# The third set of chain tiles moves from a place of the weight ring into two landing buffers

## The chip, the cores and the metric

The kernel runs on one core of one Trainium2 chip. The metric is device time in microseconds (us) of one execution, the median of the runs shown. TensorE is PE in the rows (PEld is its weight load), VectorE is DVE, ScalarE is ACT, GpSimd is POOL and SyncE is SP; SPq is SyncE issuing DMAs.

## The reference

Two transformer-like blocks over 256 tokens of width 2048, all in float32: attention and convolution with a gated FFN first, then a layer of stick-breaking attention and pooling, then an RWKV-7 layer. The change lies in the last layer, where the projection `g` is computed while the recurrence runs:

```python
r = (xr @ w_r).astype(f32)
k = (xk @ w_k).astype(f32)
v = (xv @ w_v).astype(f32)
g = (xg @ w_g).astype(f32)
...
def step(state, inp):
    r_t, w_t, k_t, v_t, kk_t, a_t = inp
    sa = jnp.einsum('bhvk,bhk->bhv', state, -kk_t)
    state = (state * w_t[:, :, None, :]
             + sa[..., None] * (kk_t * a_t)[:, :, None, :]
             + v_t[..., None] * k_t[:, :, None, :])
    return state, jnp.einsum('bhvk,bhk->bhv', state, r_t)
...
o = ((o - mean) * lax.rsqrt(var + GN_EPS)).reshape(B_, S, D) * gn_w + gn_b
bonus = jnp.sum(r * k * r_k, axis=-1, keepdims=True) * v
o = (o + bonus.reshape(B_, S, D)) * jax.nn.silu(g)
return o.astype(x.dtype) @ w_o
```

## The kernel before

**Units.** All weight matrices are streamed through one pipeline in the order of `ORDER`. A unit is a block of 512 rows by 256 columns of a weight, 512 KB, and there are 760. Four units in a row of the same 256 columns make a slab of `w_g`. The units of `w_v` end at 695, `w_g` is 696 to 727 (slabs of four: 696 to 699, 700 to 703 and so on), `w_o` is 728 to 759. `W1` is 696, the first unit of `w_g`.

**A unit's way.** SyncE lands it in one of the landing buffers `raw0` to `raw2` with two DMAs of 256 KB (line 542, in `sync_program`). ScalarE rounds it to a high part `wH` (line 573), VectorE subtracts to get the low part `wL` (`wL = raw - wH`, line 1168), and TensorE multiplies both parts with the activations. I call the ScalarE and the VectorE step together the split of a unit. A landing buffer may be filled again when both steps of the unit that it held are done: `sync_program` waits on the counts `hi` and `lo`. `wH` and `wL` form a ring of four places (`RING`), and a split has to wait until TensorE has finished the unit that held the place (`unit`).

**Who splits what, when.** Each engine runs a program written in the order of the units. At unit `u` ScalarE and VectorE first call `split(u)`, which covers the units from `SPLIT[u - 1]` to `SPLIT[u]`; then they do their part of the scan. With the full ring, `split(u)` covers unit `u + 3`. All five queues are in order, so an engine that waits at a split does nothing that stands behind it.

**The scan.** The recurrence runs as three interleaved chains of jobs and norms (`_chains`, `job`, `norm`, `turn`), spread over the `w_g` units: TensorE puts the matmuls of turns between those of the unit, and ScalarE and VectorE copy and correct what these give. Each chain has a set of tiles (`places`): `j0` and `j0b` for the first, `j1` and `j1b` for the second, both in a block that is free by then, and `j2` and `j2b` for the third, which lie where place 3 of the ring is (`wH[3]`, `wL[3]`). While chain 2 works, the ring has therefore three places: in `_slots`, `allowed` is `range(3)` and `ahead` is 2, so that `split(u)` covers only unit `u + 1`, for `u` from 695 to 721. At unit `OPEN` = 722 the ring opens again: VectorE splits unit 723 ahead of the turns of that unit and 724 behind them, and at `LAST_NORM` = 723 units 725 and 726. ScalarE waits there for chain 2 to end (`jp2`, `jd2`, lines 570 to 572) before it writes place 3. A slab's sum is taken out of PSUM at its last unit (`empty_g`, ScalarE line 624, then VectorE), and since chain 2 has the other half of those banks, all slabs of `w_g` but the last use the same one.

**Lines that the prediction follows.** On ScalarE: 573 (split), 1074 and 1076 (the first copies of a job), 1080 (copy of the bonus), 1084 (copy that TensorE's `j` by `j0b`, `j1b` or `j2b` matmuls read), 1087, and 1098 to 1104 (norm: square, table load, logarithm, exponential). On VectorE: 1168 (split and most two-operand work), 1827 and 1174 (mean of `j1b` and so on, and its subtraction), 1931 to 1933 (clearing of tiles before the scan).

Of the kernel before, what the change touches and what calls it, by code (L numbers as in the profile page):

```python
# [12 lines left out]
P = 128  # L13
# [115 lines left out]
W0, WS, W1 = U0["w_k"], U0["w_v"] + 16, U1["w_v"]  # L129
MORE_RAW = 2  # L130


def _landings():

    held, uses, out = [-1] * (RAW + MORE_RAW), [0] * (RAW + MORE_RAW), []
    for u, (n, _) in enumerate(UNITS):
        if is_whole(n):
            continue
        more = U0["w_out"] <= u < U1["w_down"]
        k = min(range(RAW + MORE_RAW if more else RAW), key=lambda q: held[q])  # L140
        uses[k] += 1
        out.append((k, uses[k], held[k]))
        held[k] = len(out) - 1
    return out


LANDING = _landings()


OPEN = U1["w_g"] - 6  # L150


def _slots():
# [3 lines left out]
    for u in range(NU):  # L157
        allowed = range(3) if W1 <= u < OPEN else range(RING)
        ahead = 2 if W1 - 1 <= u < OPEN else 3 if u in (0, OPEN) else RING
        while len(slot) < min(u + ahead, NU):  # L160
            i = len(slot)
            if whole_unit(i):
                k = (i - W0) // 2 % RING
                first = i - (i - W0) % 2
                prior.append(i - 8 if i - 8 >= W0 and whole_unit(i - 8) else max([q for q in range(first) if slot[q] == k], default=-1))
            else:
                k = min(range(3) if W1 <= i and u < OPEN else allowed, key=lambda q: held[q])
                if held[k] >= u:
                    break
                prior.append(held[k])  # L170
            held[k] = i
            slot.append(k)
# [134 lines left out]
def build_block(nc, d, out):  # L307
    ctx = ExitStack()
    with ctx:
# [158 lines left out]
        def scratch(name, shape):  # L468
# [8 lines left out]
                  (blk("j1", 0, 8192, [P, 1024]), blk("j1b", 0, 12288, [P, 1024]), mt[1]),  # L477
                  (at("j2", ring0 + 4096 * (RAW + 3), [P, 1024]),
                   at("j2b", ring0 + 4096 * (RAW + RING + 3), [P, 1024]), rsA)]
        kb = [stage, rsBU]  # L480
# [37 lines left out]
        def sync_program(e):  # L518
# [3 lines left out]
            for i, (n, ku) in enumerate(UNITS):  # L522
# [4 lines left out]
                else:  # L527
# [5 lines left out]
                    elif k >= RAW:  # L533
                        e.wait_ge(s["c_l"], 8)
                    to, done = raw[k].rearrange("p (k n) -> p k n", k=4), s[f"raw{k}"]
                cols = slice(256 * (sl % 2), 256 * (sl % 2) + 256)
# [16 lines left out]
        def scalar_program(e):  # L553
# [7 lines left out]
            def split(u):  # L561
                for i in range(SPLIT[u - 1] if u else 1, SPLIT[u]):
# [5 lines left out]
                    if PRIOR[i] >= 0:  # L568
                        e.wait_ge(s["unit"], PRIOR[i] + 1)
                    if SLOT[i] == RING - 1 and PRIOR[i] < W1 <= i:  # L570
                        e.wait_ge(s["jp2"], BASE[2][-1][0])
                        e.wait_ge(s["jd2"], BASE[2][-1][2])
                    e.copy(wH[SLOT[i]], raw[k].rearrange("p (k n) -> p k n", k=4)).then_inc(s["hi"], 1)  # L573
# [592 lines left out]
        def vector_program(e):  # L1166
# [41 lines left out]
            def stream(name, empty, tiles=None, turn=None, behind=None):  # L1208
                for u in range(U0[name], U1[name]):
                    if u == OPEN:  # L1210
                        split_units(SPLIT[u - 1], SPLIT[u - 1] + 1)
                    elif u not in WITHIN and U0[name] not in EARLY and u != LAST_NORM:
                        split(u)
# [4 lines left out]
                    if turn:  # L1218
# [4 lines left out]
                        for t in range(turn_at(u), before_last):  # L1223
                            turn(t)
                    if u == OPEN:
                        split_units(SPLIT[u - 1] + 1, SPLIT[u])
                    if u == LAST_NORM:
# [702 lines left out]
            e.wait_ge(s["unit"], W1)  # L1930
            e.memset(sets[1]["UV"], 0.0).then_inc(s["zero"], 1)
            e.memset(sets[2]["M2"], 0.0).then_inc(s["zero"], 1)
            e.memset(sets[2]["UV"], 0.0).then_inc(s["zero"], 1)
# [770 lines left out]
```

## Time and profile before

| | us |
|---|---|
| Median of 3 runs | 2452.48 |
| Lowest and highest run | 2449.43, 2454.14 |
| Span of the profiled execution | 2450.7 |
| PE busy | 2410.2 (98%) |
| DVE busy | 1662.5 (68%) |
| ACT busy | 1205.4 (49%) |
| Weight landings as a share of the DMA engines' span (q1) | 51.8% |

For the profiled execution the profile gives its span and no other time. The page's busy share is an average over all stages. For the change, the stage of `w_g` counts: it begins when TensorE ends unit 695, at about 2141 us, and ends with unit 727, at about 2340 us. In a timeline row the columns are the start, the duration, the engine, the line, the operation with out<-in, and, in brackets, how long the engine had stood idle before it and what released it.

### The profile page before, as it was taken

Reading aid. Unit: us, or ns where it says so; the run is one execution under the profiler, and the core shown is the slowest. Engines: PE = TensorE matmul, PEld = TensorE weight load, DVE = VectorE, ACT = ScalarE, POOL = GpSimd, SP = SyncE. Lnnn points to the kernel's source line nnn. Section 1 sums busy time; section 2 is a strip of 40 time slices with the busy share of each in tenths; the row PEclk is TensorE's granted clock in tenths of the full one; section 3 lists DMA queues with packets and bytes.
Section 4 is the critical chain, followed back from the end, with each engine's and each line's share of the span. In section 5 each row is a group of like instructions: output and inputs, shape, how many; then the busy total and the mean of one; then the engine's idle time right before and its main releaser. Section 6 shows DMA issues by size and latency. Waiting matters only on the chain.

```text
span 2450.7 us, 38457 instructions
## 1 busy us (share of the span) xinstructions
PE 2410.2 (98%) x15462; PEld 2088.1 (85%) x15462; DVE 1662.5 (68%) x2230; ACT 1205.4 (49%) x1595; POOL 75.3 (3%) x101
## 2 busy tenths in 40 slices
PE   9999999999999999999999999999999999999997
PEld 7888888888788888888888788888898888888786
DVE  6988888775866656665444756675754767677666
ACT  5444554654644444444444455554568301555654
POOL 0000000000000000000000000000000201021000
PEclk9999999999999999999999999999999999999999
DMA  7565456566456565656555555555743556522363
GB/s 256 190 192 169 155 178 193 181 207 192 152 184 195 180 198 183 194 181 199 189 189 180 155 181 171 167 174 183 223 141 99 165 168 209 177 80 87 121 216 128
DMA packets 420354, 427.71 MB, mean 175 GB/s; under 512 B 25600, under 2 KB 414720, under 8 KB 419472
## 3 DMA queue, kind: packets, MB, share of 16 engines
q1 hardware_dynamic: 414736, 402.53, 51.8%
q0 software_dynamic: 5008, 22.19, 2.9%
q8 instruction: 122, 2.00, 0.3%
q10 hardware_dynamic: 432, 0.53, 0.1%
q14 instruction: 56, 0.46, 0.1%
HBM read 415.19 MB, written 9.96 MB: 173 GB/s over the span
## 4 chain that ended last, share of the span: by engine, by line
PE 84%; DVE 8%; ACT 4%; DMA 2%; issue 1%; SPq 0%; ACTq 0%; DVEq 0%
PE GP L2101 78%; PE SB L2101 5%; DVE wL L1168 2%; ACT wH L573 1%; DMA raw<-w_in_dram 1%; DVE y L1168 1%; DVE wide L1168 1%; DVE x L1168 1%; DVE f L1174 1%; DMA raw<-w_o_dram 0%; PE SB L2105 0%; DVE acc L1174 0%; DVE j L1168 0%; SPq L542 0%; DVE ga L1168 0%
## 5 line engine op out<-in xcount | busy, mean ns | idle before, releaser
L1168 DVE TENSOR_TENSOR wL<-raw,wH 128x1024 fp32r<-128x1024 f32 (+1 forms) x705 | 855.8, 1224 | 473.8 <-ACT wH L573 471.7
L573 ACT CAST wH<-raw 128x1024 fp32r<-128x1024 f32 x703 | 726.9, 1047 | 496.2 <-PE GP L2101 370.7
L2101 PE MATMUL GP<-u2B,wH 128*128 128x512 f32 x1408 | 442.2, 395 | 0.0
L2101 PE MATMUL GP<-uB,wH 128*128 128x512 f32 x1152 | 361.8, 395 | 0.0
L2101 PEld LDWEIGHTS GP<-u2B,wL 128*128 128x128 f32 x1408 | 263.9, 188 | 67.9 <-DVE u2B L1174 4.8
L2101 PE MATMUL GP<-u2B,wL 128*128 128x256 f32 x1408 | 277.5, 278 | 3.0 <-DVE u2B L1174 3.0
L2101 PEld LDWEIGHTS GP<-uB,wL 128*128 128x128 f32 x1152 | 215.1, 188 | 53.6 <-DVE uB L1174 3.6
L2101 PE MATMUL GP<-xB,wH 128*128 128x512 f32 x768 | 241.2, 395 | 0.0
L2101 PE MATMUL GP<-uB,wL 128*128 128x256 f32 x1152 | 231.6, 282 | 2.5 <-DVE uB L1174 2.4
L2101 PE MATMUL GP<-hB,wH 128*128 128x512 f32 x704 | 221.1, 395 | 0.0
L2101 PEld LDWEIGHTS GP<-u2B,wH 128*128 128x128 f32 x1408 | 214.4, 189 | 0.0
L2101 PEld LDWEIGHTS GP<-uB,wH 128*128 128x128 f32 x1152 | 175.5, 189 | 0.0
L2101 PEld LDWEIGHTS GP<-xB,wL 128*128 128x128 f32 x768 | 141.8, 188 | 36.0 <-DVE xB L1168 4.0
L2101 PEld LDWEIGHTS GP<-hB,wL 128*128 128x128 f32 x704 | 132.2, 188 | 31.2
L2101 PE MATMUL GP<-xB,wL 128*128 128x256 f32 x768 | 154.9, 283 | 2.2 <-DVE xB L1168 2.2
L2101 PE MATMUL GP<-hB,wL 128*128 128x256 f32 x704 | 138.5, 278 | 0.0
L1174 DVE SCALAR_TENSOR_TENSOR acc<-z,vec,acc 128x256 f32<-128x256 f32 x240 | 115.6, 482 | 4.6
L2101 PEld LDWEIGHTS GP<-xB,wH 128*128 128x128 f32 x768 | 117.0, 189 | 0.0
L2101 PE MATMUL GP<-xr,dw 128*128 128x256 f32 x512 | 114.5, 385 | 0.0
L2101 PEld LDWEIGHTS GP<-xr,dw 128*128 128x128 f32 x512 | 97.8, 192 | 14.3 <-issue 0.5
L2101 PEld LDWEIGHTS GP<-hB,wH 128*128 128x128 f32 x704 | 107.2, 189 | 0.0
L2101 PE MATMUL GP<-xk,dw 128*128 128x256 f32 x384 | 84.5, 380 | 2.3 <-DVE xk L1174 2.3
(427 smaller groups left out, 3288.6 us busy)
## 6 DMA issues: line engine op xcount, KB each, us to landing
raw<-w_gate_up_dram SPq DMA_DIRECT2D x352, 256.0 KB, 3.7
raw<-w_in_dram SPq DMA_DIRECT2D x288, 256.0 KB, 3.4
raw<-ev_w_in_dram SPq DMA_DIRECT2D x192, 256.0 KB, 3.4
raw<-w_down_dram SPq DMA_DIRECT2D x176, 256.0 KB, 3.4
raw<-w_out_dram SPq DMA_DIRECT2D x64, 256.0 KB, 3.7
raw<-ev_w_out_dram SPq DMA_DIRECT2D x64, 256.0 KB, 3.5
dw<-w_r_dram SPq DMA_DIRECT2D x64, 256.0 KB, 3.4
raw<-w_g_dram SPq DMA_DIRECT2D x64, 256.0 KB, 3.3
```

Of the source, the lines that this page charges most:

```text
L573: e.copy(wH[SLOT[i]], raw[k].rearrange("p (k n) -> p k n", k=4)).then_inc(s["hi"], 1)
L1168: return e.tensor_tensor(o, a, b, op)
L1174: return e.scalar_tensor_tensor(out=o, in0=a, scalar=s_, in1=b, op0=op0, op1=op1)
L2101: return e.matmul(o, l, r, start=start, stop=stop, skip_group_check=True)
```

## The change

It moves `j2` and `j2b` to `raw1` and `raw2`. The ring of split weights keeps its four places all the way, so `split(u)` covers unit `u + 3` in `w_g` too. The special order at `OPEN` and ScalarE's wait at place 3 are gone. From unit `LENT` = 699 to unit 725 only `raw0` receives weights. VectorE clears `j2` and `j2b` when the split of unit 698, the last in `raw1` before that, is done. Units 726 (`raw2`) and 727 (`raw1`) are the first to land there again; SyncE waits for chain 2 to end before each (`jp2`, `ja2`, `jd2`).

```diff
 MORE_RAW = 2
+OPEN = U1["w_g"] - 6
+
+LENT, BACK = W1 + RING - 1, OPEN + RING
...
         more = U0["w_out"] <= u < U1["w_down"]
-        k = min(range(RAW + MORE_RAW if more else RAW), key=lambda q: held[q])
+        places = 1 if LENT <= u < BACK else RAW + MORE_RAW if more else RAW
+        k = min(range(places), key=lambda q: held[q])
...
-        allowed = range(3) if W1 <= u < OPEN else range(RING)
-        ahead = 2 if W1 - 1 <= u < OPEN else 3 if u in (0, OPEN) else RING
+        ahead = 3 if u == 0 else RING
...
-                k = min(range(3) if W1 <= i and u < OPEN else allowed, key=lambda q: held[q])
+                k = min(range(RING), key=lambda q: held[q])
...
-                  (at("j2", ring0 + 4096 * (RAW + 3), [P, 1024]),
-                   at("j2b", ring0 + 4096 * (RAW + RING + 3), [P, 1024]), rsA)]
+                  (at("j2", ring0 + 4096, [P, 1024]), at("j2b", ring0 + 8192, [P, 1024]), rsA)]
...
+                    if k and i >= BACK > LENT > UNITS_OF[prior]:
+                        e.wait_ge(s["jp2"], BASE[2][-1][0])
+                        e.wait_ge(s["ja2"], BASE[2][-1][1])
+                        e.wait_ge(s["jd2"], BASE[2][-1][2])
...
-                    if SLOT[i] == RING - 1 and PRIOR[i] < W1 <= i:
-                        e.wait_ge(s["jp2"], BASE[2][-1][0])
-                        e.wait_ge(s["jd2"], BASE[2][-1][2])
...
-                    if u == OPEN:
-                        split_units(SPLIT[u - 1], SPLIT[u - 1] + 1)
-                    elif u not in WITHIN and U0[name] not in EARLY and u != LAST_NORM:
+                    if u not in WITHIN and U0[name] not in EARLY and u != LAST_NORM:
                         split(u)
...
-                    if u == OPEN:
-                        split_units(SPLIT[u - 1] + 1, SPLIT[u])
...
             e.memset(sets[1]["UV"], 0.0).then_inc(s["zero"], 1)
+            e.wait_ge(s["lo"], NTH[LENT])
             e.memset(sets[2]["M2"], 0.0).then_inc(s["zero"], 1)
```

**SyncE, landings of units 697 to 701.** Two DMAs make one unit; the first carries the wait on the splits of the buffer's last unit. Before:

```order
L542 DMA raw0_54<-w_g_dram 128x2x256 [waits s_lo,s_hi]
L542 DMA raw0_54<-w_g_dram 128x2x256
L542 DMA raw1_55<-w_g_dram 128x2x256 [waits s_lo,s_hi]
L542 DMA raw1_55<-w_g_dram 128x2x256
L542 DMA raw2_56<-w_g_dram 128x2x256 [waits s_lo,s_hi]
```

Now:

```order
L546 DMA raw0_54<-w_g_dram 128x2x256 [waits s_lo,s_hi]
L546 DMA raw0_54<-w_g_dram 128x2x256
L546 DMA raw1_55<-w_g_dram 128x2x256 [waits s_lo,s_hi]
L546 DMA raw1_55<-w_g_dram 128x2x256
L546 DMA raw0_54<-w_g_dram 128x2x256 [waits s_lo,s_hi]
```

Unit 699, the third here, lands in `raw0` instead of `raw2`, and so do the 26 after it: each waits for the splits of the unit directly ahead of it instead of the one three ahead.

**ScalarE, end of unit 703 to the turns of unit 705.** Names: `small1` is the slab's sum, `j0` takes a norm, `j1b` and `j2b` belong to jobs of chains 1 and 2. Before, the two casts split units 705 and 706:

```order
L1066 ACTIVATE small1_53<-small1_53 128x512 [waits s_ev]
L573 CAST wH0_59<-raw2_56 128x1024 [waits s_unit,s_raw2]
L1098 ACTIVATE j0_161<-wide_137 128x512 [waits s_ja0,s_jd0,s_ja1,s_jp0]
L573 CAST wH1_60<-raw0_54 128x1024 [waits s_unit,s_raw0]
L1100 ACT_TABLE_LOAD
L1102 ACTIVATE j0_161<-SB1,cst_50 128x512 [waits s_jp0]
L1104 ACTIVATE j0_161<-j0_161 128x512 [waits s_ja0]
L1074 COPY j1b_164<-SB2 128x512 [waits s_jp1]
```

Now they split units 707 and 708:

```order
L1067 ACTIVATE small1_53<-small1_53 128x512 [waits s_ev]
L574 CAST wH3_62<-raw0_54 128x1024 [waits s_unit,s_raw0]
L1099 ACTIVATE j0_161<-wide_137 128x512 [waits s_ja0,s_jd0,s_ja1,s_jp0]
L574 CAST wH0_59<-raw0_54 128x1024 [waits s_unit,s_raw0]
L1101 ACT_TABLE_LOAD
L1103 ACTIVATE j0_161<-SB1,cst_50 128x512 [waits s_jp0]
L1105 ACTIVATE j0_161<-j0_161 128x512 [waits s_ja0]
L1075 COPY j1b_164<-SB2 128x512 [waits s_jp1]
```

The order stands as it was; both casts now read `raw0`, so between them VectorE must finish with the buffer and SyncE must fill it.

**VectorE, from the split of unit 697 to the first job of the scan.** Before:

```order
L1168 TENSOR_TENSOR wL1_64<-raw0_54,wH1_60 128x1024 [waits s_hi]
L1168 TENSOR_TENSOR wide_137<-GP0,wide_137 128x512 [waits s_lh]
L1168 TENSOR_TENSOR yB_134<-xr_132,yB_134 128x512 [waits s_mixh]
L1168 TENSOR_TENSOR wide_137<-GP1,wide_137 128x512 [waits s_lh]
L1689 MEMSET j1_163 128x512 [waits s_unit]
L1168 TENSOR_TENSOR yB_134<-xr_132,yB_134 128x512 [waits s_mixh] x2
L1931 MEMSET j1b_164 128x512 [waits s_unit]
L1932 MEMSET j2_165 128x512
L1933 MEMSET j2b_166 128x512
L1168 TENSOR_TENSOR j0_161<-SB0,cst_50 128x4x64 [waits s_jp0]
```

Now:

```order
L1169 TENSOR_TENSOR wL1_64<-raw0_54,wH1_60 128x1024 [waits s_hi]
L1169 TENSOR_TENSOR wide_137<-GP0,wide_137 128x512 [waits s_lh]
L1169 TENSOR_TENSOR yB_134<-xr_132,yB_134 128x512 [waits s_mixh]
L1169 TENSOR_TENSOR wL2_65<-raw1_55,wH2_61 128x1024 [waits s_hi]
L1169 TENSOR_TENSOR wide_137<-GP1,wide_137 128x512 [waits s_lh]
L1686 MEMSET j1_163 128x512 [waits s_unit]
L1169 TENSOR_TENSOR yB_134<-xr_132,yB_134 128x512 [waits s_mixh] x2
L1928 MEMSET j1b_164 128x512 [waits s_unit]
L1930 MEMSET j2_165 128x512 [waits s_lo]
L1931 MEMSET j2b_166 128x512
L1169 TENSOR_TENSOR wL3_66<-raw0_54,wH3_62 128x1024 [waits s_hi]
L1169 TENSOR_TENSOR j0_161<-SB0,cst_50 128x4x64 [waits s_jp0]
```

The splits of units 698 and 699 now stand ahead of the scan's first work; before, that of 698 stood behind it.

## Rows read from the trace of the kernel before

**Rows 1.** The page: span, and busy us, share and instructions of the engines.

```profile
span 2450.7 us, 38457 instructions
PE 2410.2 (98%) x15462; PEld 2088.1 (85%) x15462; DVE 1662.5 (68%) x2230; ACT 1205.4 (49%) x1595; POOL 75.3 (3%) x101
```

**Rows 2.** Waits of PE, 2100 to 2390 us: total us, times, longest us.

```profile
PE GP L2101 <- DVE wL L1168: 4.4, 2, 2.4
...
PE SB L2101 <- DVE j1b L1931: 0.5, 1, 0.5
```

**Rows 3.** Timeline of PE: the two matmuls behind the long waits.

```profile
2308.90 0.50 PE L2101 MATMUL GP<-yB,wL 128*128 128x256 f32 x2 [1.98 <-DVE wL L1168]
...
2330.07 0.50 PE L2101 MATMUL GP<-yB,wL 128*128 128x256 f32 x2 [2.39 <-DVE wL L1168]
```

**Rows 4.** Windows: stretch, length, busy us by engine, PEclk, DMA share, GB/s.

```profile
2141.00:2321.00 180.00, 175.80 (x2207) 145.92 (x2205) 124.65 (x201) 102.64 (x172) 31.24 (x41) 0.99 0.29 95
2310.00:2314.00 4.00, 4.00 (x37) 2.77 (x37) 0.00 (x0) 2.32 (x5) 0.00 (x0) 0.57 1.01 361
2330.50:2334.50 4.00, 4.00 (x15) 3.40 (x14) 3.14 (x5) 2.72 (x5) 0.00 (x0) 0.57 0.70 203
```

**Rows 5.** Timeline: VectorE's split of unit 701, SyncE's two DMAs for unit 704.

```profile
2169.73 1.76 DVE L1168 TENSOR_TENSOR wL<-raw,wH 128x1024 fp32r<-128x1024 f32 x1 [2.39 <-ACT wH L573]
...
2171.57 1.38 SPq L542 DMA_DIRECT2D raw<-w_g_dram  x2
```

**Rows 6.** Line 542, 2171.5 to 2172.5 us: these DMAs, duration in ns, landing in us.

```profile
L542 SPq DMA_DIRECT2D raw<-w_g_dram x2: 540/671/802, 2171.6 to 2172.2; - x2
...
DMA to landing us min/median/max: 2.9/3.2/3.4
```

**Rows 7.** Splits by tile, 2141 to 2321 us: ns min/median/max, first and last start.

```profile
L573 ACT CAST wH<-raw x27: 1029/1047/1056, 2142.5 to 2319.6; 128x1024 fp32r<-128x1024 f32 x27
...
L1168 DVE TENSOR_TENSOR wL<-raw,wH x26: 1216/1225/1771, 2150.9 to 2319.7; 128x1024 fp32r<-128x1024 f32 x26
```

**Rows 8.** Timeline of DVE at the start of the scan.

```profile
2141.61 0.69 DVE L1168 TENSOR_TENSOR wide<-GP,wide 128x512 f32<-128x512 f32 x1 [0.42 <-ACT wide L624]
...
2145.12 0.48 DVE L1933 MEMSET j2b<- 128x512 f32 x1
2145.52 3.57 DVE L1168 TENSOR_TENSOR j<-SB,cst 128x256 f32<-128x256 f32 x8
```

**Rows 9.** Timeline of ACT, end of unit 703 and units 704 and 705.

```profile
2195.97 1.04 ACT L573 CAST wH<-raw 128x1024 fp32r<-128x1024 f32 x1
...
2197.44 1.03 ACT L573 CAST wH<-raw 128x1024 fp32r<-128x1024 f32 x1
2198.49 1.28 ACT L1100 ACT_TABLE_LOAD   x1
2202.83 0.69 ACT L1102 ACTIVATE j<-SB,cst 128x512 f32<-128x512 f32 x1 [3.06 <-PE SB L2101]
...
2204.09 0.57 ACT L1074 COPY j1b<-SB 128x512 f32<-128x512 f32 x1
...
2205.29 0.59 ACT L1074 COPY j2b<-GP 128x512 f32<-128x512 f32 x1
```

**Rows 10.** Timeline of DVE in the same stretch.

```profile
2197.04 1.77 DVE L1168 TENSOR_TENSOR wL<-raw,wH 128x1024 fp32r<-128x1024 f32 x1 [0.53 <-ACT wH L573]
...
2204.22 0.69 DVE L1168 TENSOR_TENSOR wide<-wide,j 128x512 f32<-128x512 f32 x1 [0.31 <-ACT j L1104]
```

**Rows 11.** Timeline of PE: the two readers of these copies' results.

```profile
2206.01 0.59 PE L2101 MATMUL SB<-mt,cst 128*128 128x256 f32 x2
2206.44 0.59 PE L2101 MATMUL GP<-small,cst 128*128 128x256 f32 x2
```

**Rows 12.** Timelines of ACT and PE in unit 713: a copy and its reader.

```profile
2259.42 0.61 ACT L1084 COPY j2b<-GP 64x256 f32<-64x256 f32 x2
...
2260.09 0.68 PE L2101 MATMUL GP<-wide,S 64*64 64x64 f32 x16 [0.30 <-ACT j2b L1084]
```

More of the change, by code:

```diff
@@ L147 @@
 LANDING = _landings()
-OPEN = U1["w_g"] - 6
+UNITS_OF = [u for u in range(NU) if not is_whole(UNITS[u][0])]
 def _slots():
```

## The prediction

> **What bounds the kernel now.** I read the page first: PE is busy for 2410.2 of 2450.7 us [rows 1], so only what stops or slows TensorE, or lets it stop less, moves the end. The waits of PE around `w_g` come next. The largest entry is `wL` with 4.4 us in two waits; clearing `j1b` costs 0.5 us [rows 2]. The timeline places the two: 1.98 us ahead of 2308.90, unit 721, and 2.39 us ahead of 2330.07, unit 725 [rows 3]. In both, VectorE reaches the split of the next unit too late, as `split(u)` covers only `u + 1`. TensorE's granted clock falls right behind each: over the 4 us from 2310.00 and from 2330.50 it averages 0.57 [rows 4]. With x the share of the stretch at the lower level (1.2 instead of 2.4 GHz), 1 - x/2 = 0.57, x = 0.86, so 3.4 us at half speed and 1.7 us lost, each time. All of this is what a split three units ahead can give back: 1.98 + 2.39 + 2 x 1.7 = **7.8 us**. Over the rest of the stage TensorE hardly stops: 175.8 of 180 us from 2141 to 2321 [rows 4]. TensorE is there kept busy by units and turns alternately, and its turns need copies of ScalarE and corrections of VectorE just ahead of their use.
>
> **Part one, the ring.** Four places instead of three remove both waits on `wL`: `split(u)` now makes unit `u + 3`, three units ahead of need. Instruction counts stay as they are: 32 splits for the 32 units of `w_g`. Gain 7.8 us, if nothing else stops TensorE in these places.
>
> **Part two, the start.** Two splits move from behind the scan's first work to ahead of it on VectorE, those of units 698 and 699. VectorE has no free time there: clearing `j2b` ends at about 2145.5 us and the first evacuations start at 2145.52, and last 3.57 us for eight [rows 8]. One split takes 1.22 us [rows 7]. The first falls ahead of the evacuation at 2141.61, where VectorE stands idle for 0.42 us [rows 8], and so costs 0.8 us, which delays the clearing of `j1b`, for which TensorE already waited [rows 2]; the second costs another 1.25 us. The evacuations start 2.0 us later, and TensorE's transposes of the jobs write where these read. I charge **2.0 us**. Its bounds: 0.8 (only the wait for `j1b` grows) and 2.45 (two splits whole).
>
> **Part three, one landing buffer.** From unit 699 to 725 a unit's landing starts when VectorE has finished the unit ahead of it, not the one three ahead. The rows for one refill: VectorE's split of unit 701 ends at 2169.73 + 1.76 = 2171.49; the DMAs are issued from 2171.57, the second some 0.7 us later, and land 2.9 to 3.4 us after issue [rows 5, 6]. From the end of `wL` to data is 2171.57 - 2171.49 + 0.6 + 3.4 = **4.1 us**. Adding the ScalarE step (1.05) and the VectorE step (1.22) [rows 7], one round takes 6.4 us if both engines are ready at once. Before, a landing lay ready for long, as three buffers took turns.
>
> The 27 splits of ScalarE start from 2142.5 to 2319.6 us [rows 7], 26 steps of 6.8 us. So the loop just fits if nothing is added. But each step sits in an in-order queue behind the scan's work, and the scan's work sits behind it. In the trace the steps are uneven: ScalarE splits at 2195.97 and at 2197.44 [rows 9], 1.5 us apart, where the new loop needs 6.4. The later of such a pair waits, and so does all that ScalarE has behind it.
>
> I walk through that place, in times of the trace before. The first cast of the pair ends at 2197.0, VectorE's `wL` of it runs 2197.04 to 2198.81 [rows 10]. The refill is there 4.1 us later, at 2202.9; the second cast ends at 2203.95. ScalarE then loads its table (1.28), so the logarithm starts at 2205.25 instead of 2202.83: **2.4 us late** [rows 9]. The 3.06 us that ScalarE stood idle ahead of it are the cover, and it is gone. Behind it, each by 2.4 us: the exponential, VectorE's `wide` at 2204.22, which already waits for it [rows 10], and the copies of `j1b` (2204.09 + 0.57 = 2204.66) and `j2b` (2205.29 + 0.59 = 2205.88). TensorE wants the results of the two at 2206.01 and 2206.44 [rows 9, 11]: slack 1.35 and 0.56 us. So it stops for 1.1 us at the first and, at 2205.88 + 2.4 against 2206.44 + 1.1, for 0.75 us at the second, **1.9 us** in all.
>
> The same walk, carried on with the delays that it produced, gives for TensorE: unit 699, 1.15 (`j0b` of line 1084 behind the split of 702); 700 to 704, nothing, as these delays lengthen the time until the next split and the loop catches up; 705, 1.9; 707, 2.7 (line 1084 again, behind a table load); 711, 0.4; 713, 3.2; 717, 2.2; 721, 2.0. Unit 713 is the clearest: line 1084's copy starts at 2259.42 and TensorE has already waited 0.30 us for it at 2260.09 [rows 12]; no slack at all, so what the loop adds there, it pays. Sum: 1.15 + 1.9 + 2.7 + 0.4 + 3.2 + 2.2 + 2.0 = **13.6 us**. Bounds: 0, if the copies find cover that I don't see, and 22 us: a step longer than 6.4 us by a queued 0.8 on average, 27 x (6.4 + 0.8) = 194 us against the 177 us that 26 steps take now, and two more stops of 2 to 3 us.
>
> The Trainium skill, "DMA: Bandwidth & Descriptors", section "Rules for kernel authors", says to issue a DMA early, compute, and wait late, so that its fixed cost overlaps. That speaks against this change, whose loads are issued at the last moment. Its section "Anatomy of one DMA" fits about 2.0 us plus the bytes at 436 GB/s for another issuing path, 2.6 us for 256 KB. As an estimate from that page, the refill would be 0.1 + 0.6 + 2.6 = 3.3 us instead of 4.1 and the stops of the scan would shrink by 0.8 us in each of seven places, 5.6 us in all. The row has 2.9 to 3.4 us for these very DMAs, and I go by it.
>
> **The clock.** TensorE's clock fell after the stops of 1.98 and 2.39 us [rows 3, 4]. Four of the new stops (2.7, 3.2, 2.2, 2.0) are of that size. Each fall costs 1.7 us, unless TensorE is waiting anyway. I count two of four, **3.4 us**; bounds 0 and 6.8.
>
> **The end.** Units 726 and 727 land only when chain 2 has ended. Its last norm is done some 12 us later than before, about 2334 in the changed kernel, the landing takes 4.1 us, and TensorE needs unit 726 after 2342. No stop. ScalarE and VectorE have one split fewer at 722 and 723. `w_o` starts with its landings as before.
>
> **Sum.** -7.8 + 2.0 + 13.6 + 3.4 = **+11.2 us**. The span would be 2461.9 us instead of 2450.7. The median of the runs is 1.8 us over the span (2452.48), so the forecast is 2452.5 + 11.2 = 2463.7; the walk rounds against the change in some steps, and I say **2463 us**.
>
> **The rivals.**
> First, the loop is hidden. If copies and corrections find cover, only the gain and the start remain: -7.8 + 2.0 = -5.8, 2446.7 us; down to 2444.7 without the start. For it: ScalarE has idle time ahead of what it does in the scan, as the 3.06 us here [rows 9], and the loop's 6.4 us is under the mean step of 6.8. Against it: pairs 1.5 us apart. It decides at the second cast of a pair: the logarithm of unit 705 must start no more than about 0.56 us late.
> Second, half of it is hidden: 13.6 / 2 = 6.8 and no fall of the clock, so -7.8 + 2.0 + 6.8 = +1.0, 2453.5 us, no change that can be seen.
> Third, the loop rules all of the stage. If each of the rounds takes 7.2 us or more, with a fall of the clock at each large stop: -7.8 + 2.0 + 17 + 6.8 = +18, 2470.5 us; with the upper bound of part three 2475. For it: each stop leaves the engines' work in bunches, and I saw rounds of 9 and 10 us in the walk.
> Fourth, the change may not do what it says: if the two old waits on `wL` stayed, as VectorE is late for all things, the gain of 7.8 would be missing. Against it: the units in question are split two units earlier in program order. It would add to the third.
>
> **How the numbers follow.** A measurement of this kernel can tell about 0.2%, 4.9 us, from no change. Forecast (+5 to +15): 0.52. Hidden loop: 0.12. Half hidden: 0.14. Loop rules all, with the fourth: 0.22. Faster 0.11, same 0.16, slower 0.73 (a little of the forecast falls within 0.2%). The range runs from 2448 us, which leaves most of the hidden loop out, to 2473, which cuts the tail of the third; about 0.18 lies outside. The forecast's own range is 2457 to 2468.
>
> **What would show it.** Right: PE has no wait on `wL` in `w_g` any more; ScalarE's idle time ahead of line 573 is put down to the landing of `w_g` (or to SPq), over 27 splits some 30 us; the splits are never less than 6.4 us apart; PE waits for copies of lines 1074 and 1084 in units 705, 707 and 713; the evacuations at 2145.5 come 2 us later; `w_g` ends 8 to 15 us later than 2340. Wrong: refills of clearly less than 4.1 us; ScalarE waiting long but TensorE not; or the two waits on `wL` at the end of `w_g` still there. Most in doubt is how much of ScalarE's lateness reaches TensorE; one us of slack more per place would halve the sum.

## The result, and the profile after

Both kernels were run side by side on one chip.

| | before | after |
|---|---|---|
| Median, us | 2452.42 | 2472.93 |
| Lowest and highest run, us | 2449.43, 2454.14 | 2469.63, 2478.66 |
| Span of the profiled execution, us | 2450.7 | 2471.3 |

The ratio is 1.009 with a 95% interval of 1.0078 to 1.0101: **20.5 us slower**. The forecast was 2463 us, from a sum of 11.2 us, with a range up to 2473. The sign is as forecast, the size is nearly twice it, and the time lies just inside the range's upper end.

The page of the kernel after, its span and the busy us of its engines (to [rows 1]):

```profile
span 2471.3 us, 38458 instructions
PE 2411.9 (98%) x15462; PEld 2088.1 (84%) x15462; DVE 1663.0 (67%) x2230; ACT 1205.3 (49%) x1595; POOL 76.3 (3%) x101
```

No engine has more work than before: the busy times differ by 1.7 us at most. The 20.6 us of span are waits and time at a lower clock. Line numbers of the kernel after are shifted by a few: TensorE's helper is L2099 and L2103, ScalarE's split L574, VectorE's L1169, and the copies of a job L1075 to L1088. The waits of PE from 2141 to 2420 us (to [rows 2]; total us, times, longest us):

```profile
PE SB L2099 <- ACT j0b L1085: 6.6, 3, 3.2
PE SB L2099 <- ACT j1b L1085: 5.3, 2, 2.6
PE GP L2099 <- ACT j2b L1085: 2.5, 1, 2.5
...
PE GP L2099 <- DVE wL L1169: 1.3, 2, 0.9
...
PE SB L2099 <- DVE j1b L1928: 0.9, 1, 0.9
```

`wL` has left the top of the list: the two waits of 1.98 and 2.39 us are gone, and the 1.3 us that remain lie in other units. In their place TensorE waits 14.4 us for the scan's copies of line 1085. What holds these up is one row further, in the waits of ACT from 2141 to 2341 us:

```profile
ACT wH L574 <- DMA raw<-w_g_dram: 69.6, 19, 7.1
```

and in SyncE's, in the same stretch, the wait before a landing:

```profile
SPq L532 <- DVE wL L1169: 161.1, 26, 10.2
```

Here ScalarE stands for 69.6 us in front of a landing buffer that is being filled, and SyncE stands for 161.1 us until VectorE has emptied it. The window of [rows 4] in one row, and TensorE's four slow places (to [rows 4]; length, busy us by engine, PEclk, DMA share, GB/s):

```profile
2141.00:2321.00 180.00, 163.82 (x1996) 135.88 (x1994) 114.13 (x185) 89.60 (x152) 30.16 (x37) 0.97 0.25 81
2227.00:2230.40 3.40, 3.40 (x64) 3.17 (x62) 3.27 (x5) 0.37 (x1) 0.00 (x0) 0.50 0.13 44
2257.70:2261.10 3.40, 3.40 (x62) 3.17 (x60) 1.44 (x3) 1.59 (x4) 0.00 (x0) 0.50 0.47 148
2305.50:2308.90 3.40, 3.40 (x58) 3.05 (x57) 2.07 (x3) 0.66 (x3) 1.39 (x2) 0.50 0.35 111
2336.20:2339.60 3.40, 3.40 (x45) 2.96 (x41) 1.23 (x2) 2.69 (x5) 0.53 (x1) 0.50 0.57 145
```

PE is busy for 163.8 of the 180 us where it was 175.8. And the granted clock is at 0.50, its lower level, for 3.4 us behind each of four stops; in this stage of the kernel before it was so twice. The large stops in the timeline of PE, in order of time (to [rows 3]):

```profile
2166.50 0.69 PE L2099 MATMUL SB<-j,j0b 128*64 128x64 f32 x16 [1.15 <-ACT j0b L1085]
...
2210.52 0.70 PE L2099 MATMUL SB<-mt,cst 128*128 128x256 f32 x2 [1.01 <-ACT j1b L1075]
2211.73 0.70 PE L2099 MATMUL GP<-small,cst 128*128 128x256 f32 x2 [0.52 <-ACT j2b L1075]
...
2226.04 0.68 PE L2099 MATMUL SB<-wide,S 64*64 64x64 f32 x16 [2.63 <-ACT j1b L1085]
...
2256.89 0.68 PE L2099 MATMUL SB<-wide,S 64*64 64x64 f32 x16 [2.28 <-ACT j0b L1085]
...
2276.06 0.68 PE L2099 MATMUL GP<-wide,S 64*64 64x64 f32 x16 [2.54 <-ACT j2b L1085]
...
2305.31 0.98 PE L2099 MATMUL SB<-wide,S 64*64 64x64 f32 x16 [2.62 <-ACT j1b L1085]
...
2335.16 0.68 PE L2099 MATMUL SB<-wide,S 64*64 64x64 f32 x16 [3.21 <-ACT j0b L1085]
```

The place that the prediction walked through, in the timeline of ACT after (to [rows 9]):

```profile
2199.39 1.05 ACT L574 CAST wH<-raw 128x1024 fp32r<-128x1024 f32 x1
...
2206.28 1.05 ACT L574 CAST wH<-raw 128x1024 fp32r<-128x1024 f32 x1 [5.32 <-DMA raw<-w_g_dram]
2207.35 1.28 ACT L1101 ACT_TABLE_LOAD   x1
2208.64 0.69 ACT L1103 ACTIVATE j<-SB,cst 128x512 f32<-128x512 f32 x1
...
2209.90 0.57 ACT L1075 COPY j1b<-SB 128x512 f32<-128x512 f32 x1
```

Two casts that stood 1.5 us apart now stand 6.9 us apart. The second waits 5.32 us for its landing, and behind it the table load, the norm and the copies wait too, though their inputs are there. TensorE pays 1.01 + 0.52 = 1.53 us for it, and 1.9 were predicted.

To see where the time comes in, I took from each trace the times at which TensorE reports units as done, counted from its report of unit 695, and subtracted those of before. The table gives the time by which each kernel is then later (negative: earlier). The scan's work at the end of a unit stands behind the unit's report, so a stop in unit 707 shows at 708. The rows below the first belong to the experiments.

| Kernel | 698 | 704 | 708 | 712 | 714 | 718 | 721 | 724 | 725 | 727 | 729 | 743 |
|---|---|---|---|---|---|---|---|---|---|---|---|---|
| after | 1.7 | 3.3 | 10.0 | 13.7 | 16.0 | 20.1 | 16.3 | 22.3 | 18.0 | 19.8 | 21.9 | 20.5 |
| e10: after again | 2.1 | 3.7 | 9.0 | 12.9 | 16.3 | 20.7 | 16.8 | 23.6 | 19.4 | 21.2 | 23.2 | 22.6 |
| e1: old ring, one buffer | 0.0 | 1.4 | 7.9 | 8.9 | 12.5 | 16.8 | 16.7 | 28.6 | 24.9 | 24.9 | 26.4 | 25.6 |
| e2: old ring, two buffers | 0.0 | 0.0 | 0.0 | 0.0 | 0.0 | 0.0 | -0.1 | 0.7 | -0.8 | -0.8 | 0.7 | 0.7 |
| e8: ring of four, one buffer | 1.6 | 2.5 | 8.6 | 12.4 | 14.3 | 18.4 | 14.5 | 21.8 | 17.6 | 17.9 | 19.9 | 19.3 |
| e3: ring of four, two buffers | 1.8 | 1.5 | 1.9 | 1.9 | 1.9 | 1.9 | -2.0 | -2.1 | -6.3 | -6.3 | -4.4 | -4.5 |
| e4: e3 with a late start | 0.0 | 2.6 | 3.0 | 2.9 | 2.9 | 2.9 | -0.9 | -1.0 | -5.2 | -5.2 | -3.3 | -3.9 |
| e9: e3 with a later lead | 0.0 | 0.7 | 1.1 | 1.1 | 1.1 | 1.1 | -2.7 | -2.8 | -7.0 | -7.0 | -5.1 | -5.8 |
| e5: after, half of the load | 1.8 | 1.8 | 6.4 | 6.2 | 7.2 | 9.1 | 5.3 | 7.7 | 3.5 | 5.4 | 7.4 | 6.8 |
| e6: after, four DMAs | 1.8 | 3.1 | 9.3 | 12.8 | 14.6 | 18.6 | 14.8 | 20.0 | 15.8 | 17.6 | 19.6 | 17.9 |
| e7: after, 726 and 727 in `raw0` | 1.8 | 3.6 | 8.8 | 9.9 | 13.5 | 17.8 | 13.9 | 19.5 | 15.3 | 22.3 | 22.8 | 21.7 |

### The profile page after: what moved, and what is told of

Read it like the earlier page. It is cut to its first block, busy times and chain, and to the rows that moved or that the text cites. A ratio compares the mean times of both kernels' runs of the same rounds, so it can differ in the third digit from the quotient of the medians.

```text
span 2471.3 us, 38458 instructions
## 1 busy us (share of the span) xinstructions
PE 2411.9 (98%) x15462; PEld 2088.1 (84%) x15462; DVE 1663.0 (67%) x2230; ACT 1205.3 (49%) x1595; POOL 76.3 (3%) x101
## 4 chain that ended last, share of the span: by engine, by line
PE 82%; DVE 8%; ACT 4%; DMA 3%; issue 1%; SPq 0%; ACTq 0%; DVEq 0%
PE GP L2099 77%; PE SB L2099 5%; DVE wL L1169 2%; ACT wH L574 2%; DMA raw<-w_g_dram 2%; DMA raw<-w_in_dram 1%; DVE wide L1169 1%; DVE y L1169 1%; DVE x L1169 1%; DVE f L1175 1%; DVE j L1169 0%; DMA raw<-w_o_dram 0%; SPq L546 0%; PE SB L2103 0%; DMA raw<-w_v_dram 0%
## 5 line engine op out<-in xcount | busy, mean ns | idle before, releaser
L1169 DVE TENSOR_TENSOR wL<-raw,wH 128x1024 fp32r<-128x1024 f32 (+1 forms) x705 | 856.8, 1225 | 510.9 <-ACT wH L574 509.2
L574 ACT CAST wH<-raw 128x1024 fp32r<-128x1024 f32 x703 | 727.2, 1047 | 567.8 <-PE GP L2099 371.5
L2099 PE MATMUL GP<-u2B,wH 128*128 128x512 f32 x1408 | 442.2, 395 | 0.0
L2099 PE MATMUL GP<-uB,wH 128*128 128x512 f32 x1152 | 361.8, 395 | 0.0
L2099 PEld LDWEIGHTS GP<-u2B,wL 128*128 128x128 f32 x1408 | 263.9, 188 | 67.9 <-DVE u2B L1175 4.9
L2099 PE MATMUL GP<-u2B,wL 128*128 128x256 f32 x1408 | 277.5, 278 | 3.0 <-DVE u2B L1175 3.0
L2099 PEld LDWEIGHTS GP<-uB,wL 128*128 128x128 f32 x1152 | 214.9, 188 | 54.9 <-DVE uB L1175 3.0
L2099 PE MATMUL GP<-xB,wH 128*128 128x512 f32 x768 | 241.2, 395 | 0.0
L2099 PE MATMUL GP<-uB,wL 128*128 128x256 f32 x1152 | 231.6, 282 | 2.9 <-DVE uB L1175 2.6
L2099 PE MATMUL GP<-hB,wH 128*128 128x512 f32 x704 | 221.1, 395 | 0.0
L2099 PEld LDWEIGHTS GP<-u2B,wH 128*128 128x128 f32 x1408 | 214.3, 189 | 0.0
L2099 PEld LDWEIGHTS GP<-uB,wH 128*128 128x128 f32 x1152 | 175.5, 189 | 0.0
L2099 PEld LDWEIGHTS GP<-xB,wL 128*128 128x128 f32 x768 | 141.8, 188 | 36.1 <-DVE xB L1169 4.0
L2099 PEld LDWEIGHTS GP<-hB,wL 128*128 128x128 f32 x704 | 132.2, 188 | 31.2
L2099 PE MATMUL GP<-xB,wL 128*128 128x256 f32 x768 | 154.9, 283 | 2.2 <-DVE xB L1169 2.2
L2099 PE MATMUL GP<-hB,wL 128*128 128x256 f32 x704 | 138.5, 278 | 0.0
L2099 PEld LDWEIGHTS GP<-xB,wH 128*128 128x128 f32 x768 | 117.0, 189 | 0.0
L2099 PE MATMUL GP<-xr,dw 128*128 128x256 f32 x512 | 112.8, 381 | 0.0
L2099 PEld LDWEIGHTS GP<-xr,dw 128*128 128x128 f32 x512 | 96.6, 190 | 13.8 <-issue 0.5
L2099 PEld LDWEIGHTS GP<-hB,wH 128*128 128x128 f32 x704 | 107.2, 189 | 0.0
L2099 PE MATMUL GP<-xk,dw 128*128 128x256 f32 x384 | 84.5, 380 | 2.3 <-DVE xk L1175 2.3
```

The lines of the kernel that those rows point to most:

```text
L1169: return e.tensor_tensor(o, a, b, op)
L2099: return e.matmul(o, l, r, start=start, stop=stop, skip_group_check=True)
```

## The experiments

The theory was that of the prediction: with one landing buffer, a refill and the two steps of a split follow one another, and the in-order queues of ScalarE and VectorE carry each late landing over to the scan. The first rival was that the four places of the ring do it: a split made three units ahead comes at worse moments. The second was that the place of `j2` and `j2b`, or SyncE's new waits at the end, do it.

### One landing buffer alone, two alone (e1, e2)

The kernel before keeps its ring and its tiles, and only gives up landing buffers for units 699 to 725:

```diff
-        k = min(range(RAW + MORE_RAW if more else RAW), key=lambda q: held[q])
+        places = 1 if U1["w_v"] + 3 <= u < U1["w_g"] - 2 else RAW + MORE_RAW if more else RAW
+        k = min(range(places), key=lambda q: held[q])
```

> The kernel before with one part of the change alone: from unit 699 to 725 only raw0 receives weights; set 2 stays in place 3 of the ring, the ring has three places there. Theory (one landing buffer makes a loop of 6.4 us whose waits stand ahead of the scan's copies): all of the loss and none of the gain. The trace of the changed kernel shows 16 us of stops for copies and four falls of the clock (6.8 us) against two before, and the two waits on wL stay or grow as a split is only one unit ahead: 2452.4 + 16 + 3.4 = 2472 us or more, ScalarE waiting some 70 us for landings of w_g. Rival (the four places in the ring, and the two splits ahead of the scan, cost the time): no loss here, 2452 us.

It took **2475.12 us**, 1.010 times before (1.0085 to 1.0116). That is 2 us more than the change itself, which has the gain of the ring on top. The waits of ACT and of PE, 2141 to 2341 us:

```profile
ACT wH L574 <- DMA raw<-w_g_dram: 61.8, 18, 6.3
```

```profile
PE GP L2102 <- DVE wL L1169: 6.4, 2, 4.4
PE SB L2102 <- ACT j1b L1085: 5.4, 2, 2.7
```

The same copies are late as in the kernel after. With the old ring the last waits on `wL` grow too, to 4.4 us, as there is no split in reserve. Its stop in unit 711 is only 0.62 us, for which the next section has the reason.

e2 differs in one number, `places = 2`:

> As the run with one landing buffer, but raw0 and raw1 receive the weights of units 699 to 725, raw2 none. Theory: a landing now starts when the unit two ahead is split, so one round covers two units, 3.2 us a unit against steps of 6.8 us; only pairs of splits 1.5 us apart can still wait, under 1 us each: 2452 to 2455 us, ScalarE waiting under 15 us for landings of w_g. Rival (any buffer taken away lengthens the stage in proportion): half of the loss with one, 2462 us.

It took **2451.16 us**, ratio 1.0002 (0.9993 to 1.0012): no difference. Up to unit 720 its times agree with before to 0.03 us. The largest wait of PE, 2141 to 2341 us, is the old one:

```profile
PE GP L2102 <- DVE wL L1169: 5.0, 3, 2.4
```

Of ScalarE the same view has 0.2 us, once, for a landing. So in this stage the third buffer was not needed; the second is what hid the refill.

### The ring of four with two buffers, and with one (e3, e8)

To have the ring of four and a second buffer, `j2` needs another home. In the order of `vec` and `cst` I brought together vectors and constants that nobody reads any more in this stage, and put `j2` there. `j2b` stays in `raw2`.

```diff
-        places = 1 if LENT <= u < BACK else RAW + MORE_RAW if more else RAW
+        places = 2 if LENT <= u < BACK else RAW + MORE_RAW if more else RAW
...
-                  (at("j2", ring0 + 4096, [P, 1024]), at("j2b", ring0 + 8192, [P, 1024]), rsA)]
+                  (at("j2", vec0 + 4 * (VEC["w_dw"][0] + 64), [P, 1024]), at("j2b", ring0 + 8192, [P, 1024]), rsA)]
```

> The changed kernel with j2 moved once more, from raw1 to constants and vectors that nothing reads any more in w_g (their order is changed so that they lie side by side); j2b stays in raw2. Units 699 to 725 land in raw0 and raw1, the ring keeps four places. Theory: the gain of the ring without the loop: -7.8 (both waits on wL and their clock falls) + 2.0 (start) = 2446.6 us; no PE wait on wL from 2141 to 2340 us. Rival (the ring of four is what costs, by its waits for TensorE and its split ahead of the scan): 2465 us or more, as the changed kernel.

It took **2446.01 us**, 0.9979 times before (0.9969 to 0.9988), and is the version that beats both kernels: 4.7 us faster than before in the same runs (2450.67). A second set of runs (e11) gave 2448.07 us, 0.9985 (0.9976 to 0.9994). Against the kernel after, with its two sets (2472.93 and 2472.99), that is 25 to 27 us. In the table it starts 1.8 us late, stays there, gains 3.8 us at unit 721 and 4.2 us at 725. Its waits of ACT, 2141 to 2341 us:

```profile
ACT wH L574 <- PE GP L2099: 24.6, 14, 3.4
```

ScalarE waits at its splits here too, 24.6 us, but for TensorE to free a place of the ring. PE has no large stop from it, and the window over the stage shows its busy time and clock (columns as above):

```profile
2141.00:2321.00 180.00, 176.26 (x2215) 146.58 (x2214) 127.25 (x203) 105.56 (x174) 32.49 (x41) 1.00 0.31 101
```

e8 is e3 with `places = 1` and nothing else:

> The kernel with two landing buffers and four places in the ring, with one edit: one landing buffer for units 699 to 725. Everything else stays (j2 in the old constants). Theory (the number of landing buffers alone makes the difference): the time of the changed kernel, 2472 us. Rival (j2 lying in raw1, or the late release of raw1, matters): nearer to 2446.

It took **2469.67 us**, 1.0072 (1.0057 to 1.0087). One number moves 24 us, with the tiles where they were in e3. This excludes the rival of the ring. It also excludes that of `j2`'s place as the cause of the loss; the intervals of e8 and of the kernel after overlap, so the 3 us between them may be nothing.

### How much the refill weighs (e5, e6)

e5 takes away half of the load. Of each unit from 699 to 725 only the first of the two DMAs is issued, so half of these weights is left out of the result.

```diff
-                for j in range(2):
+                for j in range(1 if LENT <= i < BACK else 2):
```

> The changed kernel with only the first of the two DMAs of each unit from 699 to 725 (left out: half of the weights of these 27 units; all splits and matmuls stay). The refill is shorter by one issue and its landing's lag, from some 4.1 to 3.4 us. Theory (the refill, in a loop with both splits, sets the stops): each of the seven or eight places with a stop of 1 to 3.2 us gets 0.7 us shorter, 5 to 6 us, and one or two falls of the clock (1.7 us each) go: 2464 us, with SalarE's wait for w_g landings down from 73 to some 50 us. Rival (the stops come from how late VectorE and ScalarE are in their own queues): no change, 2472 us.

It took **2456.93 us**, 1.0022 (1.0012 to 1.0031), 16 us less than the kernel after (13.7 between the two traces). The refill, from the end of VectorE's split to the landed data, has a median of 3.03 us instead of 4.07. So about 1 us of refill in 27 rounds is worth 16 us, more than half of what the loop costs. The waits of ACT and PE, 2141 to 2341 us:

```profile
ACT wH L574 <- DMA raw<-w_g_dram: 51.4, 16, 6.5
```

```profile
PE SB L2099 <- ACT j1b L1085: 3.5, 2, 1.8
PE SB L2099 <- ACT j0b L1085: 2.5, 1, 2.5
```

The stops for copies of line 1085 shrink from 2.63, 2.54, 2.62 and 3.21 us to 1.74, 1.31, 1.76 and 2.48, and that of unit 711 (2.28) is gone. The expectation was 7 us too high: it had the stops 5 to 6 us shorter and one or two falls of the clock fewer. Over the seven places of the prediction the trace has some 8 us less of stops, and one fall in this stage where the kernel after has four.

e6 was meant as the other direction, a longer refill: four DMAs of 128 KB instead of two of 256 KB.

```diff
-                for j in range(2):
+                for j in range(4 if LENT <= i < BACK else 0):
+                    e.dma_start(to[:, j:j + 1, :],
+                                d[name][sl // 2, 2 * ku + j // 2].rearrange("p (k n) -> p k n", k=2)[:, j % 2:j % 2 + 1, cols]).then_inc(done, 16)
+                for j in range(0 if LENT <= i < BACK else 2):
```

> The changed kernel with four DMAs of 128 KB instead of two of 256 KB for each unit from 699 to 725: two more issues of 0.6 us, a refill of some 5.3 instead of 4.1 us, a round of 7.6 instead of 6.4 us. Theory: the mean step between splits in the kernel before is 6.8 us, so nearly every round pays and the cost is no longer confined to a few places: between 27 x (7.6 - 6.8) = 22 us and 27 x 1.2 = 32 us more than the changed kernel, 2493 to 2503 us. Rival (queues of the engines): within 5 us of 2472.

That was a miss: **2469.42 us**, 1.0072 (1.0055 to 1.0089), 3.5 us under the kernel after instead of 22 to 32 us over it. The two intervals overlap, so the gain itself is not certain; that there is no loss is. The issue rows of SyncE, of the kernel after and then of e6 (durations in ns, then landing in us):

```profile
L546 SPq DMA_DIRECT2D raw<-w_g_dram x51: 539/612/1637, 2140.5 to 2329.6; - x51
...
DMA to landing us min/median/max: 2.9/3.2/4.6
```

```profile
L542 SPq DMA_DIRECT2D raw<-w_g_dram x100: 327/432/1513, 2146.6 to 2328.0; - x100
...
DMA to landing us min/median/max: 2.2/2.3/3.7
```

I had taken four issues at the price of today's two each. A smaller DMA is issued in 0.43 us instead of 0.61 and lands in 2.3 us instead of 3.2. Four of them make a refill of 3.82 us (median), shorter than 4.07. So e6 is no test of a longer refill. It fits the loop's theory (a refill a little shorter, a stage no longer), but it is e5 that shows it.

### The end (e7)

In the kernel after, units 726 and 727 wait for chain 2 to end. In e7 they land in `raw0`, whose waits are only on `hi` and `lo`:

```diff
-LENT, BACK = W1 + RING - 1, OPEN + RING
+LENT, BACK = W1 + RING - 1, U1["w_g"]
```

> The changed kernel, but units 726 and 727 land in raw0 as well, so no weight waits for chain 2 before w_o. The trace of the changed kernel shows 3.1 us of delay in units 723, 726 and 727 which the prediction had not. Theory A (they come from the lateness of the engines after the loop, the landings of 726 and 727 were there 5 to 8 us before their casts): no gain, 2472 to 2475 us. Rival B (the wait for chain 2 holds them up): 2 to 3 us faster, 2470.

It took **2473.0 us**, 1.0089 (1.0074 to 1.0104), no different from the kernel after. It was 2.8 us ahead of it at unit 725 (its stop at unit 711 was 1.07 us) and 2.5 us behind at 727, as units 726 and 727 now wait in the loop as well. At 2356.30 TensorE waits 4.60 us for `wL` of unit 727. The loop, carried on, costs more at the end than the wait for chain 2. e7 can't tell what that wait costs by itself, as it puts another one in its place. The trace of the kernel after can: the data of 726 was there 3.8 us before its cast, as shown under "The end" below.

### The start (e4, e9)

Two splits ahead of the scan's first work cost 1.7 us. In e4 the lead of e3 grows to three units only behind the scan's start:

```diff
-        ahead = 3 if u == 0 else RING
+        ahead = {0: 3, W1 - 1: 3, W1: 2, W1 + 1: 2, W1 + 2: 2, W1 + 3: 3}.get(u, RING)
...
-            e.wait_ge(s["lo"], NTH[LENT])
+            e.wait_ge(s["lo"], NTH[W1] + 1)
```

> As the run before, but the splits of units 698 and 699 stay behind the first work of the scan: the ring works one unit ahead up to unit 698 and takes up the lead of three units at 699 and 700. Theory: this takes away the 2.0 us that the two splits cost at the start: 2444.6 us, VectorE's first evacuation of the scan starts at 2145.5 us after the start as in the kernel before. Rival (the start is hidden by TensorE's own work, or the double splits at 699 and 700 cost as much): same time as the run before.

It took **2446.42 us**, 0.9987 (0.9978 to 0.9996), no gain over e3. The start cost is gone (0.0 at unit 698), but 2.6 us are there by 702: where the lead grows, ScalarE has two splits in a row, and the second one's landing is not there (timelines of ACT and PE in e4):

```profile
2156.46 1.05 ACT L574 CAST wH<-raw 128x1024 fp32r<-128x1024 f32 x1
2161.16 1.04 ACT L574 CAST wH<-raw 128x1024 fp32r<-128x1024 f32 x1 [3.65 <-DMA raw<-w_g_dram]
```

```profile
2162.79 0.39 PE L2099 MATMUL SB<-j,j0b 128*64 128x64 f32 x6 [0.94 <-ACT j0b L1085]
```

It is the mechanism of the change in small: a split in front of a copy, and a landing behind the split.

In e9 the lead grows to two units at 701 and to three at 703:

```diff
-        ahead = {0: 3, W1 - 1: 3, W1: 2, W1 + 1: 2, W1 + 2: 2, W1 + 3: 3}.get(u, RING)
+        ahead = {0: 3, W1 - 1: 3}.get(u, 2 if W1 <= u < W1 + 5 else 3 if W1 + 5 <= u < W1 + 7 else RING)
```

> As the run with a late start, but the lead grows from one unit to three at 701 and 703 instead of by two splits in a row at 699 and 700. In the late-start run ScalarE waited 3.65 us for the landing of the second of two splits in a row, and TensorE 0.94 us for the j0b copy behind it. Theory: without that pile-up the start costs neither this nor the 1.5 us of the run with two landing buffers: 1 to 2.5 us faster than both, 2444 us. Rival (VectorE must do the two extra splits somewhere in the scan, and it costs the same wherever): 2446 us.

It took **2446.06 us**, 0.998 (0.9971 to 0.9989). That was a miss too: 2444 us had been expected, 1 to 2.5 us under both. Its trace is 0.7 us ahead of e3's at unit 727 and 1.2 us at 743; the medians can't tell the two apart.

### The same kernels again (e10, e11)

> The changed kernel again, unedited, on the chip of the runs beside it: 1.009 of the kernel before, 2472 us. If the run with j2 in the old constants and one landing buffer (ratio 1.0072) is truly 3 us faster, this shows 1.0085 or more; if chips differ, it shows 1.007 to 1.008.

The kernel after once more: **2472.99 us**, 1.0086 (1.0072 to 1.01).

> The kernel with two landing buffers and four places in the ring again, with more rounds and on one chip with the changed kernel: 0.998 of the kernel before, with the interval below 1, and 25 us under the changed kernel.

e3 once more, with the result given above. The two repeats show how much of one trace can be relied on. The stops of the kernel after come at the same instructions and differ by some 0.3 us at most. Its clock does not fall at the same ones. In e10 (windows, columns as above):

```profile
2224.00:2228.00 4.00, 4.00 (x100) 3.69 (x101) 2.96 (x5) 2.28 (x6) 0.00 (x0) 1.00 0.32 110
...
2272.30:2276.30 4.00, 4.00 (x55) 3.56 (x56) 3.86 (x7) 1.32 (x2) 1.70 (x2) 0.69 0.07 21
```

Behind the stop of unit 707, 2.80 us long here, the clock stays up, and behind that of 713, 2.22 us long, it falls. In the first trace it was the other way round. Four falls came in both, but the last one of e10, at 2331.9, lasted 6.8 us and not 3.4.

## Why the prediction was right in sign and short in size

**The waits on `wL` (part one): right.** 7.8 us were predicted. The table shows -3.8 at unit 721 (from 20.1 at 718) and -4.2 from 724 to 725 (22.25 to 18.04) in the kernel after, 8.0 us in all, and 8.2 in e3 from 718 to 725.

**The start (part two): right.** 2.0 us predicted, 1.7 measured, with the stop for `j1b` grown from 0.5 to 0.9 us; the evacuations start at 2147.16 instead of 2145.52.

**The refill (part three): right in its median.** 4.1 us predicted, median 4.07. (The text has the second DMA some 0.7 us behind the first and the sum 0.6; [rows 6] have 0.6.) The Trainium skill's "DMA: Bandwidth & Descriptors", section "Anatomy of one DMA", would have made it 3.3 us by the prediction's estimate; its formula is for another issuing path, and the trace does not bear it out here. The section "Rules for kernel authors" of the same page of the Trainium skill (issue early, wait late) agrees with e1 against e2: 25 us and nothing.

**The stops of the scan (part three): the places right, three sizes wrong.** In us:

| Unit | 699 | 705 | 707 | 711 | 713 | 717 | 721 or 722 | sum |
|---|---|---|---|---|---|---|---|---|
| Predicted | 1.15 | 1.9 | 2.7 | 0.4 | 3.2 | 2.2 | 2.0 | 13.6 |
| Measured | 1.15 | 1.53 | 2.63 | 2.28 | 2.24 | 2.62 | 3.21 | 15.7 |

(713 measured is 2.54 less the 0.30 that it had before.) Unit 713 came 1.0 us shorter and 721 1.2 us longer than predicted, which nearly cancel. The step of the walk that failed most is that for unit 711, 0.4 predicted and 2.28 measured. The walk took the loop at its shortest there, and two things lengthened it. In the timeline of DVE, then in the row of SyncE's two DMAs behind it, then in ACT:

```profile
2248.74 1.22 DVE L1169 TENSOR_TENSOR wL<-raw,wH 128x1024 fp32r<-128x1024 f32 x1
```

```profile
L546 SPq DMA_DIRECT2D raw<-w_g_dram x2: 540/576/613, 2250.0 to 2250.6; - x2
...
DMA to landing us min/median/max: 3.2/3.9/4.6
```

```profile
2255.26 1.04 ACT L574 CAST wH<-raw 128x1024 fp32r<-128x1024 f32 x1 [7.12 <-DMA raw<-w_g_dram]
2256.21 0.63 ACT L1085 COPY j0b<-SB 64x256 f32<-64x256 f32 x2
```

VectorE could have begun at 2247.36, when the cast was done, and began at 2248.74, behind four operations on `wide`; and the second DMA landed after 4.6 us instead of 3.2. Together 2.8 us, where a stop of 0.4 had been forecast. Other runs separate the two. In e7, the same program up to this unit, and in e1, VectorE was late too, but the second DMA landed after 3.5 us, and the stops were 1.07 and 0.62 us; in e10 it landed after 4.7 us, and the stop was 2.42 us. Why some landings here took over 1 us longer stays open.

The mean round, from one `wL` to the next, came out as 7.6 us, half of the rounds at 7.1 or less and the longest at 11.0. The forecast had reckoned with 6.4 where both engines are ready and with 6.8 available on average. The third rival put its own point at 7.2 us or more, and 2472.93 lies between its two prices, 2470.5 and 2475. That is in part luck. Its 17 us set 27 rounds of 7.2 us against 26 steps; like for like they are 26 x (7.2 - 6.8) = 10.4 us, and its price would have been 2464. And TensorE stopped in the few places of the walk, not all through the stage. The rival with the fourth was given 0.22; a large loss should have had more, as the walk had already shown rounds of 9 and 10 us.

**The clock: the price nearly right, the count wrong.** A fall is 3.4 us at half speed, and 1.7 us were charged for it. The unit times allow a check: from unit 707 to 708 the kernel after loses 4.18 us, of which 2.63 are the stop and 1.55 the fall; the other three falls come out at 1.51 to 1.54 us in the same way. Where the clock stayed up, the loss is the stop: 2.24 us in unit 713, and 2.88 for the stop of 2.80 in unit 707 of e10. I counted two falls of four candidates, 3.4 us. There were four, 6.1 us: the stop of 711 became a fifth candidate, and one of the five had none. No run keeps the stops and the clock up throughout.

**The end: wrong.** I charged 0. In units 723, 726 and 727 the kernel after loses 1.3, 0.6 and 1.2 us, 3.1 in all. At 729 it loses another 2.0, and at 736, where before stopped for 1.52 us itself, it gets 1.3 back: 3.8 us net. The failed step is "the landing takes 4.1 us, and TensorE needs unit 726 after 2342. No stop." It priced when the data of 726 arrives, and not when ScalarE and VectorE get to it. In rows after: SyncE's DMAs of 725, then those of 726, then ACT.

```profile
L546 SPq DMA_DIRECT2D raw<-w_g_dram x2: 540/942/1345, 2335.9 to 2336.5; - x2
...
DMA to landing us min/median/max: 3.3/4.8/6.3
```

```profile
L546 SPq DMA_DIRECT2D raw<-w_g_dram x2: 539/578/618, 2341.3 to 2341.9; - x2
...
DMA to landing us min/median/max: 3.0/3.1/3.2
```

```profile
2342.78 1.05 ACT L574 CAST wH<-raw 128x1024 fp32r<-128x1024 f32 x1 [3.70 <-DMA raw<-w_g_dram]
...
2348.91 1.03 ACT L574 CAST wH<-raw 128x1024 fp32r<-128x1024 f32 x1
```

The landing of unit 725 took up to 6.3 us, and its cast waited 3.70 us for it, to 2342.78. Unit 726 was issued at 2341.3, when chain 2 had ended, and was there by 2341.9 + 3.2 = 2345.1; its cast began only at 2348.91, without a wait for it, behind a norm that stands behind the cast of 725 in ScalarE's queue. (For that norm's first step, line 1099, TensorE stopped for 1.12 us at 2344.41, the loss in unit 723.) So it was the backlog in the queues, from the last round of the loop, and not the wait for chain 2, that made 726 late. The 2.0 us at 729 are something else. TensorE waits there for `gv`, in the kernel after and in e3:

```profile
2364.70 0.51 PE L2099 MATMUL GP<-oyB,wL 128*128 128x256 f32 x2 [1.77 <-DVE gv L1169]
```

```profile
2337.05 0.50 PE L2099 MATMUL GP<-oyB,wL 128*128 128x256 f32 x2 [1.67 <-DVE gv L1169]
```

e3, which has no loop, loses 1.9 us there as well, and e2 1.6. What brings this wait was not tried.

**The sum.** -8.0 + 1.7 + 15.7 + 6.1 + 3.8 = 19.3 us, and 1.3 us in small waits between units 699 and 706 make 20.6. Against the forecast of 11.2, the end has 3.8 more, the clock 2.7, the stops 2.1 and the small waits 1.3; the start and the gain have 0.5 less. So the terms that failed are the end put at nothing, the clock's two falls where four came, and the walk's 0.4 us for unit 711. The mechanism, a late landing carried over to the scan by queues that are in order, was right.

**The rivals.** The hidden loop (2446.7) is what e3 does with a second buffer, at 2446.01: its price was right for a kernel that was not built. That the waits on `wL` would stay was wrong. Of what was to be seen, the copies of 1075 and 1085 in 705, 707 and 713, the later start and the missing waits on `wL` came. The shortest distance of two casts in the loop, 6.3 us, was near the 6.4 named. Two came in another size: ScalarE's wait for landings was put at 30 us and was 69.6, and `w_g` ended 19.8 us later and not 8 to 15.

## What to carry to other kernels

When a load buffer is taken away, compare the whole loop (end of the last reader, issue, landing, each reader in its own queue) with the shortest distance between two uses in program order, not with the mean: here 6.4 us against a mean of 6.8 looked as if it fitted, and cost 24 us (e8 against e3), while a second buffer made it free. What stands behind a wait in an in-order queue pays for it, so price a late load by the slack of the work queued behind it. When stops are near the size of those that already brought the clock down, charge the fall to some of them: it came behind four of five here, and behind one of four in e5.

## What the runs showed of the hardware

- Two DMAs of 256 KB from one queue landed 3.2 us after issue (median) and took 0.61 us each to issue (after); four of 128 KB landed in 2.3 us at 0.43 us each (e6). To fill 512 KB into a waiting buffer, the four were ready 0.25 us earlier (3.82 against 4.07 us).
- TensorE's clock did not always fall behind a stop of the same size. In the kernel after, it fell behind stops of 2.28, 2.62, 2.63 and 3.21 us and not behind 2.54. In e10 it fell behind 2.22 and not behind 2.80. In e2 it fell behind 1.98 and not behind 2.39, and in e5 behind 1.74 and not behind 2.48. In these stages a fall mostly lasted 3.4 us at 0.50; one of e10 lasted 6.8 and one of e1, from 2337.7, 13.7 us.
- Single landings of the same kind took up to 4.6 us inside the stage and 6.3 us at its end, where GpSimd's transfer of `g` (512 KB, issued at 2336.86) runs at the same time; in e7 the same pair gave 5.8 us. That the one is the cause of the other was not tried.
